# The retention stage of a two-block transformer kernel, rebuilt

## The chip, the cores and the metric

One NeuronCore of a Trainium2 chip runs the whole kernel in one launch. The metric is device time in microseconds; the median of three runs of the kernel before is 1687.16 us (1682.4 to 1688.15).

## What is computed

The reference applies two blocks to 256 tokens of width 1024, batch 1, in float32. The first has two layers (grouped plus dilated attention, then latent attention, each with an MLP); the second has two layers with SwiGLU feeds around a mixer: differential attention, then retention. The change is in the retention:

```
def _retention(xn, w_in, subln, w_out):        # 4 heads, Dk 256, Dv 512
    q, k, v, g = split(xn @ w_in)
    ...                                        # chunks of 128; over all 256 tokens the same as:
    # o[q] = sum over keys <= q of (q.k / 16) * gamma**(q - key) * v[key]
    o = _rms(o, subln)                         # over the 512 of a head
    return (silu(g) * o) @ w_out
x1 = h + 0.5 * _swiglu(_rms(h, ...), ...)      # feed "swi2" ends here
m  = _retention(_rms(x1, mix_norm), ...)       # norm 8 of the kernel, then "rt_in", "rt_out"
x2 = x1 + m                                    # norm 9, feed "swi3"
```

## The kernel before

All weights are packed on the host into 267 slabs of 128 x 2048 float32 (1 MB each). SyncE brings them in order into a ring of six (`raw`), as subtractions free its places. Each slab is split into a high part `whi` (ScalarE cast to fp32r, L236) and a low part `wlo` (VectorE subtraction, L240), rings of three. `split_high(m)` waits until slab m - 3 is used up. Activations are split the same way (`xh`, `xl`), and every product is taken as three fp32r matmuls (`three`, L246 to L248). An input slab holds 256 output columns, 48 matmuls of 256 columns; an output slab holds 256 rows of the second matrix, 24 matmuls of 512 columns into the four `accs` banks. The engines run their lists in the order in which the code is written, coupled by semaphores; there is no scheduler.

Between two stages stands a norm, numbered q. In a "raw" norm (q in `RAW_Q`) the residual times the gain is transposed and split at once, the root of the mean square is worked out beside it, and the scale is applied later (`scale_out`, `rstd`). Norm 8 is not one of them: `scale_block` (L579) waits for the root, multiplies, and only then PE transposes (`turn_part`, L481); `first_slabs` starts the retention's first slab by features. `last_slabs` is the end of a stage's output slabs; in raw norms it takes six more matmuls of the older slab before it waits for the newest operand. Norm 5, ahead of the attention stage `da_in`, is raw and starts with `first_tokens` (tokens as rows).

`rt_in` has 24 slabs, six per head: q, k, two of v, two of g. `rt_tensor` projects each into one of six PSUM banks, q, k and g with features as rows, v with tokens as rows; VectorE copies q, k, v out (L2339, L2342), ScalarE takes Silu of g (L2325). The first head's rest is written out, the other three are a loop. When all 24 are done, `ret_tensor` starts. For each head u: `scores` (fp32, L2355), VectorE multiplies by the decay table (`decayed`, L2443), 12 products of 128 columns with v (L2402) that give o with features as rows, ScalarE squares (L2421), PE sums over features with a column of ones (L727), ScalarE takes the root (L2424), PE spreads it along the rows (L734), VectorE scales, applies the gate and splits (L2454, L2457, L2465, L2472), PE runs two output slabs (`out_`). Head u + 1's products and scores stand ahead of head u's output slabs in PE's list. The last two output slabs go through `last_slabs`.

## Time and profile before

| | |
|---|---|
| runs | 1687.16, 1688.15, 1682.4 us |
| the profiled execution | 1686.48 us, its span 1684.7 us |
| granted TensorE clock, mean | 0.992 |
| busy share of PE, DVE, ACT | 98%, 63%, 50% |
| chain of waits that ended last | PE 86%, DVE 7%, ACT 4% |

PE is TensorE's matmuls, DVE VectorE, ACT ScalarE, POOL GpSimd. A busy share is a mean over all stages; what one stage is limited by is seen only in windows and timelines of that stage. One fp32 matmul shows as two records on PE, an fp32r matmul or a transpose as one. Records overlap their neighbours, so the pace of a row of matmuls is read from their starts.

### The profile page before, as it was taken

The numbers are of one execution on the slowest core, as the hardware profiler recorded it, in microseconds if no ns is written. First come the engines' busy times: TensorE is split into PE (matmuls) and PEld (weight loads), VectorE is DVE, ScalarE is ACT, GpSimd is POOL, SyncE is SP. The second block draws the span as 40 slices with busy tenths as digits, with TensorE's granted clock in tenths as the row PEclk, the third lists the DMA queues.
The fourth block names the chain that finished last, engine by engine and source line by source line (L and its number), as shares of the span: only waits on it lengthen the run. The fifth ranks groups of instructions, "written<-read, shape, count | busy, mean of one in ns | idle before, by whom it ended". The sixth has DMA issues, their size and how long they took to land.

```text
span 1684.7 us, 24578 instructions
## 1 busy us (share of the span) xinstructions
PE 1648.3 (98%) x9684; PEld 1418.1 (84%) x9686; DVE 1061.4 (63%) x1214; ACT 846.4 (50%) x1046; POOL 32.1 (2%) x44
## 2 busy tenths in 40 slices
PE   8999999999999999999999999999999998999999
PEld 7878888758888788889888888888888998878887
DVE  6766655766665666666777666666666454566665
ACT  5654444665444454446775544544444443345443
POOL 2000000000000000000100000000000000000000
PEclk9999999999999999999999999999999999999999
DMA  9525545323554454544344545454544443335540
GB/s 368 193 116 214 179 192 200 120 92 123 203 191 182 175 191 184 200 186 176 126 163 172 212 178 200 165 210 187 195 179 169 178 189 126 125 114 212 191 183 25
DMA packets 42714, 294.19 MB, mean 175 GB/s; under 512 B 4736, under 2 KB 5040, under 8 KB 8592
## 3 DMA queue, kind: packets, MB, share of 16 engines
q1 hardware_dynamic: 39168, 281.04, 44.2%
q0 software_dynamic: 2752, 10.58, 1.8%
q10 hardware_dynamic: 720, 1.51, 0.2%
q8 instruction: 56, 0.92, 0.2%
q14 instruction: 18, 0.15, 0.0%
HBM read 289.96 MB, written 3.15 MB: 174 GB/s over the span
## 4 chain that ended last, share of the span: by engine, by line
PE 86%; DVE 7%; ACT 4%; issue 2%; DMA 1%; SPq 0%; DVEq 0%; ACTq 0%
PE ups L267 25%; PE accs L246 11%; PE accs L248 11%; PE accs L247 11%; PE ups L265 11%; DVE wlo L240 2%; PE ups L248 2%; PE ups L247 2%; PE ups L246 2%; PE ups L270 2%; ACT whi L236 1%; DVE h L719 1%; DMA raw<-weights 1%; PE ups L2402 1%; PE ups L432 1%
## 5 line engine op out<-in xcount | busy, mean ns | idle before, releaser
L240 DVE TENSOR_TENSOR wlo<-raw,whi 128x2048 fp32r<-128x2048 f32 x265 | 609.1, 2300 | 206.8 <-ACT whi L236 206.8
L267 PE MATMUL ups<-xhl,whi 128*128 128x512 f32 x1824 | 634.1, 396 | 0.0
L236 ACT CAST whi<-raw 128x2048 fp32r<-128x2048 f32 x265 | 505.3, 1909 | 113.1 <-PE accs L248 60.6
L265 PE MATMUL ups<-xhl,wlo 128*128 128x256 f32 x1596 | 445.0, 279 | 0.0
L267 PEld LDWEIGHTS ups<-xhl,whi 128*128 128x128 f32 x1824 | 331.0, 188 | 64.1
L265 PEld LDWEIGHTS ups<-xhl,wlo 128*128 128x128 f32 x1596 | 300.9, 189 | 10.1
L246 PE MATMUL accs<-whi,hidh 128*128 128x512 f32 x660 | 259.3, 393 | 1.7 <-DVE hidl L895 1.7
L248 PE MATMUL accs<-whi,hidl 128*128 128x512 f32 x660 | 257.2, 390 | 0.0
L247 PE MATMUL accs<-wlo,hidh 128*128 128x512 f32 x660 | 257.1, 390 | 0.0
L246 PEld LDWEIGHTS accs<-whi,hidh 128*128 128x128 f32 x660 | 124.0, 188 | 26.8 <-issue 4.5
L248 PEld LDWEIGHTS accs<-whi,hidl 128*128 128x128 f32 x660 | 124.0, 188 | 26.4
L247 PEld LDWEIGHTS accs<-wlo,hidh 128*128 128x128 f32 x660 | 124.1, 188 | 25.5
L246 PE MATMUL accs<-whi,xhl 128*128 128x256 f32 (+1 forms) x368 | 120.9, 329 | 4.2 <-DVE xhl L2472 2.6
L869 DVE TENSOR_TENSOR hid<-ups,hid 128x512 f32<-128x512 f32 x70 | 48.4, 691 | 121.5 <-ACT hid L842 68.2
L248 PE MATMUL accs<-whi,xhl 128*128 128x256 f32 (+1 forms) x368 | 116.9, 318 | 0.0
L247 PE MATMUL accs<-wlo,xhl 128*128 128x256 f32 (+1 forms) x368 | 116.7, 317 | 0.0
L850 ACT CAST hidh<-hid 128x512 fp32r<-128x512 f32 x76 | 47.2, 621 | 128.0 <-DVE hid L893 75.8
L842 ACT COPY hid<-ups 128x512 f32<-128x512 f32 x44 | 25.7, 585 | 131.1 <-PE ups L267 131.1
L895 DVE TENSOR_TENSOR hidl<-hid,hidh 128x512 fp32r<-128x512 f32 x76 | 52.6, 693 | 52.2 <-ACT hidh L850 52.2
L246 PEld LDWEIGHTS accs<-whi,xhl 128*128 128x128 f32 x368 | 70.4, 191 | 12.7 <-issue 3.9
L248 PEld LDWEIGHTS accs<-whi,xhl 128*128 128x128 f32 x368 | 70.3, 191 | 4.8
L847 ACT COPY sub_rstd<-ups 128x512 f32<-128x512 f32 x44 | 25.7, 584 | 96.2 <-PE ups L267 96.2
(282 smaller groups left out, 2022.1 us busy)
## 6 DMA issues: line engine op xcount, KB each, us to landing
raw<-weights SPq DMA_DIRECT2D x265, 1024.0 KB, 4.8
gain<-gains POOLq DMA_DIRECT2D x9, 512.0 KB, 4.0
rel_scratch<-sub_rstd POOLq DMA_DIRECT2D x1, 2048.0 KB, 17.6
big<-rel_scratch POOLq DMA_DIRECT2D x1, 1536.0 KB, 9.4
h<-x_in SPq DMA_DIRECT2D x2, 512.0 KB, 6.8
raw<-weights SPq DMA_DIRECT2D x2, 512.0 KB, 10.3
tabs<-consts POOLq DMA_DIRECT2D x1, 1024.0 KB, 7.7
gain<-gains ACTq DMA_DIRECT2D x1, 512.0 KB, 5.1
```

The costliest lines, as they stand in the source:

```text
L236: nc.scalar.copy(whi[:, m % SPLIT, :], raw[:, m % RAW, :]).then_inc(hi_ready, 1)
L240: nc.vector.tensor_tensor(wlo[:, m % SPLIT, :], raw[:, m % RAW, :], whi[:, m % SPLIT, :].bitcast(F32), ALU.subtract).then_inc(lo_ready, 1)
L246: nc.tensor.matmul(out_ap, sh, mh, start=first, stop=False)
L247: nc.tensor.matmul(out_ap, sh, ml, start=False, stop=False)
L248: return nc.tensor.matmul(out_ap, sl, mh, start=False, stop=last)
L265: nc.tensor.matmul(bank[:, 0:T], W(wlo, n, k, j * P, (j + 1) * P), xh[:, k, :], start=False, stop=False)
L267: mm = nc.tensor.matmul(bank, W(whi, n, k, j * P, (j + 1) * P), xhl[:, :, k, :], start=k == 0, stop=k == KC - 1)
L270: nc.tensor.matmul(bank[:, 0:T], W(wlo, n, k, j * P, (j + 1) * P), xh[:, k, :], start=False, stop=False)
L842: nc.scalar.copy(flat2(slot), sum_parts(0)[0 if begin else 1]).then_inc(S("feed_side"), 1)
L850: nc.scalar.copy(hidh[:, g % per, :, :].rearrange("p a n -> p (a n)"), slot).then_inc(S("feed_hidden_high"), 1)
L869: nc.vector.tensor_tensor(flat2(part), sum_parts(second)[0], flat2(part), ALU.add).then_inc(S("feed_sum"), 1)
L895: nc.vector.tensor_tensor(hidl[:, g % per, :, :].rearrange("p a n -> p (a n)"), slot, hidh[:, g % per, :, :].rearrange("p a n -> p (a n)") ...
```

## The change

- Norm 8 is raw and of the token kind (`RAW_Q`, `TOKEN_Q`), so `first_slabs` goes and `first_tokens` starts the stage. Since k and v then lack the norm's scale, v is multiplied by the reciprocal of the mean square (`rt_square`); q's scale falls out of the head's own norm, whose epsilon is scaled instead (`eps_raw`); the gate's Silu takes `rstd` as its scale.
- A head's slabs now come as v, v, q, k, g, g. v and g are projected with tokens as rows, q and k with features as rows, into the four `accs` banks in turn.
- Scores stand between the halves of the head's fifth slab and the value products between the halves of the sixth. The products are three of 512 columns, with o's tokens as rows, into `up[2]` and `up[3]`.
- ScalarE's Square accumulates the sum over the row (no matmuls for sum and spread). `gated` multiplies o by root and gate in one instruction per token block.
- Eight pairs of 128-feature blocks are transposed (`turn_pair`), three between halves of slabs 8, 9 and 14, five between halves of output slabs 0 to 4; ScalarE takes the high part with the gain as scale, DVE the low part.
- The loops over heads are written out on all three engines.

In the diff new functions are whole; of removed ones only the first lines stand.

```diff
@@ -72,8 +72,8 @@
-PLAIN_NORMS = (4, 9)
-ROOT_NORMS = (0, 2, 5, 6, 7, 8, 10)
+PLAIN_NORMS = (4,)
+ROOT_NORMS = (0, 2, 5, 6, 7, 8, 9, 10)
...
@@ -329,25 +329,6 @@
-        def first_slabs(pe, n, q):
...
@@ -458,10 +439,10 @@
-        TOKEN_Q = (2, 5)
-        RAW_Q = (0, 1, 2, 3, 4, 5, 6, 7, 9)
+        TOKEN_Q = (2, 5, 8)
+        RAW_Q = (0, 1, 2, 3, 4, 5, 6, 7, 8, 9)
...
-        SCALES = [0, "ab_eps", 1, 2, "c_eps", 3, 5, 6, "eps", 7, 8, 10]
+        SCALES = [0, "ab_eps", 1, 2, "c_eps", 3, 5, 6, "eps", 7, 8, 9, "r_eps", 10]
...
@@ -722,10 +703,6 @@
-        def sum_tokens(dst, squares, heads, first=True, last=True):
...
@@ -743,7 +720,7 @@
-        ROWS = {"swi0": 1, "swi1": 2, "swi2": 3, "swi3": 4 + RT_HEADS}
+        ROWS = {"swi0": 1, "swi1": 2, "swi2": 3, "swi3": 4}
...
@@ -2295,186 +2263,233 @@
+        n_ro = FIRST["rt_out"]
+        RT_SLABS = 6
+        q_rt, k_rt = big[:, 0:2 * T], big[:, 2 * T:4 * T]
+        att_rt = hid
+        v_rt, gate_rt = (big[:, at * T:(at + 8) * T].rearrange("p (s t n) -> p s t n", s=2, t=TB) for at in (4, 12))
+        on_rt = big[:, 20 * T:36 * T].rearrange("p (u t n) -> p u t n", u=RT_HEADS, t=TB)
+        rt_junk = xn[:, 0:4 * T].rearrange("p (t n) -> p t n", t=TB)
+        rt_square = sb("rt_square", [P, TB])
+        rt_sums = sb("rt_sums", [P, TB])
+        RT_PAIRS = 2 * RT_HEADS
+        def rt_bank(m):
+            return accs[:, m % 4, :]
+        def rt_high(c):
+            return hidh[:, (c % 14) // 2, c % 2, :] if c % 14 < 6 else xh[:, c - 6, :]
+        def rt_low(c):
+            return hidl[:, (c % 14) // 2, c % 2, :] if c % 14 < 6 else xl[:, c - 6, :]
+        def rt_features(s):
+            return (lambda k: rt_high(2 * s + k)), (lambda k: rt_low(2 * s + k))
+        def pair_bank(p):
+            return up[1] if p < 3 or p % 2 else up[0]
...
         def rt_tensor(pe):
...
+            def bank_free(m):
+                if m >= 4:
+                    u, j = (m - 4) // RT_SLABS, (m - 4) % RT_SLABS
+                    if j < 2:
+                        pe.wait_ge(S("rt_v"), 2 * u + j + 1)
+                    else:
+                        pe.wait_ge(S("rt_taken"), 4 * u + j - 1)
+            def half_slab(m, half_):
+                n, j = n_r + m, m % RT_SLABS
+                if half_ == 0:
+                    pe.wait_ge(lo_ready, n + 1)
+                    bank_free(m)
+                if j in (2, 3):
+                    mm = project_features(n, rt_bank(m), (half_,))
+                else:
+                    mm = project_tokens(n, rt_bank(m), blocks=(half_,))
+                if half_ == 1:
...
-        def ret_tensor(pe):
             def scores(u):
+                pe.wait_ge(S("rt_taken"), 4 * u + 2)
+                if u >= 1:
+                    pe.wait_ge(S("r_decayed"), u)
...
+                        mm = nc.tensor.matmul(up[0][:, kb * T + kb * P:(kb + 1) * T],
+                                              k_rt[:, c * T + kb * P:c * T + (kb + 1) * P],
+                                              q_rt[:, c * T + kb * P:(c + 1) * T], start=c == 0, stop=c == 1)
...
-            def sum_squares(u):
...
+            def values(u):
+                pe.wait_ge(S("r_decayed"), u + 1)
+                pe.wait_ge(S("rt_v"), 2 * u + 2)
+                if u >= 1:
+                    pe.wait_ge(S("r_gated"), u)
...
-            def spread_root(u):
...
+                    for kb in range(t + 1):
+                        at = kb * T + t * P
+                        mm = nc.tensor.matmul(up[2 + t], att_rt[:, u % 2, at:at + P], v_rt[:, u % 2, kb, :],
+                                              start=kb == 0, stop=kb == t)
+                mm.then_inc(S("r_values"), 1)
+            def turn_pair(p):
+                u = p // 2
+                pe.wait_ge(S("r_gated"), u + 1)
+                if p >= 1:
+                    pe.wait_ge(S("r_low"), p if p < 4 else p - 1)
+                for c in range(2):
+                    at = (2 * (p % 2) + c) * P
+                    for t in range(TB):
+                        mm = nc.tensor.transpose(pair_bank(p)[:, c * T + t * P:c * T + (t + 1) * P],
+                                                 on_rt[:, u, t, at:at + P], ident)
+                mm.then_inc(S("r_turned"), 1)
+            for m in range(RT_HEADS * RT_SLABS):
+                u, j = m // RT_SLABS, m % RT_SLABS
+                if m == 0:
+                    first_tokens(pe, n_r, 8, rt_bank(0)).then_inc(slab_used, 1)
+                else:
+                    half_slab(m, 0)
+                    if j == 4:
+                        scores(u)
+                    if j == 5:
+                        values(u)
+                    if m in (8, 9, 14):
+                        turn_pair((8, 9, 14).index(m))
+                    half_slab(m, 1)
+            for s in range(6):
+                n = n_ro + s
+                pe.wait_ge(lo_ready, n + 1)
+                pe.wait_ge(S("r_low"), s + 1)
+                if s == 0:
+                    pe.wait_ge(S("rt_taken"), 4 * RT_HEADS - 2)
+                project_out(n, *rt_features(s), first=s == 0, blocks=(0,))
+                if s == 0:
+                    pe.wait_ge(S("rt_taken"), 4 * RT_HEADS)
+                if s < 5:
+                    turn_pair(s + 3)
+                project_out(n, *rt_features(s), first=s == 0, blocks=(1,)).then_inc(slab_used, 1)
+            pe.wait_ge(S("r_low"), 7)
+            last_slabs(pe, n_ro + 6, rt_features(6), rt_features(7), 9,
+                       ready=lambda: pe.wait_ge(S("r_low"), RT_PAIRS))
+        def rt_scalar(act):
+            def stats(u):
+                act.wait_ge(S("r_values"), u + 1)
...
-            def out_(u):
...
+                    ins = nc.scalar.activation(rt_junk[:, t, :], up[2 + t], ACT.Square, accum_out=rt_sums[:, t:t + 1])
+                ins.then_inc(S("r_sq"), 1)
+                if u == 0:
+                    act.wait_ge(S("scale_ready"), SCALES.index("r_eps") + 1)
+                act.wait_ge(S("r_sq"), u + 1)
...
+                    act.wait_ge(S("r_rstd"), u)
+                for t in range(TB):
+                    ins = nc.scalar.activation(std8[:, 0, t:t + 1], rt_sums[:, t:t + 1], ACT.Sqrt,
+                                               bias=eps_raw[:, t:t + 1], scale=1.0 / RT_DV)
+                ins.then_inc(S("r_std"), 1)
+            def high_pair(p):
+                act.wait_ge(S("r_turned"), p + 1)
+                if p == RT_PAIRS - 1:
+                    act.wait_ge(slab_used, n_ro + 1)
+                for c in range(2):
+                    ins = nc.scalar.activation(rt_high(2 * p + c), pair_bank(p)[:, c * T:(c + 1) * T], ACT.Copy,
+                                               scale=cols[:, G_RT + 2 * p + c:G_RT + 2 * p + c + 1])
+                ins.then_inc(S("r_high"), 1)
+            raw_root_scalar(act, 9)
+            for m in range(RT_HEADS * RT_SLABS):
+                u, j = m // RT_SLABS, m % RT_SLABS
+                split_high(act, n_r + m + 2)
+                if j == 1 and u >= 1:
+                    stats(u - 1)
+                if j in (2, 3):
+                    act.wait_ge(slab_used, n_r + m + 1)
+                    if u >= 1:
+                        act.wait_ge(S("r_scores"), u)
+                    nc.scalar.copy((q_rt, k_rt)[j - 2], rt_bank(m)).then_inc(S("rt_taken"), 1)
+                if j in (4, 5):
+                    act.wait_ge(slab_used, n_r + m + 1)
+                    if m == 4:
+                        act.wait_ge(rstd_ready, ROOTS[9] + 1)
+                    if u >= 2:
+                        act.wait_ge(S("r_gated"), u - 1)
...
-        def ret_scalar(act):
...
-        def ret_vector(dve):
+                        ins = nc.scalar.activation(gate_rt[:, u % 2, t, (j - 4) * T:(j - 3) * T],
+                                                   rt_bank(m)[:, t * T:(t + 1) * T], ACT.Silu,
+                                                   scale=rstd[:, t:t + 1])
+                    ins.then_inc(S("rt_taken"), 1)
+                if m in (8, 9, 14):
+                    high_pair((8, 9, 14).index(m))
+            stats(RT_HEADS - 1)
+            for s in range(5):
+                split_high(act, n_ro + s + 2)
+                high_pair(s + 3)
+            split_high(act, n_ro + 7)
+            split_high(act, n_ro + 8)
+        def rt_vector(dve):
...
+                    ins = nc.vector.tensor_tensor(att_rt[:, u % 2, sl], up[0][:, sl], decay[:, u, sl], ALU.mult)
...
+            def gated(u):
+                dve.wait_ge(S("r_std"), u + 1)
+                nc.vector.reciprocal(rstd8[:, 0, 0:TB], std8[:, 0, 0:TB]).then_inc(S("r_rstd"), 1)
+                dve.wait_ge(S("r_rstd"), u + 1)
+                dve.wait_ge(S("rt_taken"), 4 * u + 4)
+                for t in range(TB):
+                    ins = nc.vector.scalar_tensor_tensor(on_rt[:, u, t, :], up[2 + t], rstd8[:, 0, t:t + 1],
+                                                         gate_rt[:, u % 2, t, :], ALU.mult, ALU.mult)
+                ins.then_inc(S("r_gated"), 1)
+            def low_pair(p):
+                dve.wait_ge(S("r_high"), p + 1)
+                for c in range(2):
+                    ins = nc.vector.scalar_tensor_tensor(rt_low(2 * p + c), pair_bank(p)[:, c * T:(c + 1) * T],
+                                                         cols[:, G_RT + 2 * p + c:G_RT + 2 * p + c + 1],
+                                                         rt_high(2 * p + c).bitcast(F32), ALU.mult, ALU.subtract)
+                ins.then_inc(S("r_low"), 1)
+            raw_root(dve, 9)
+            dve.wait_ge(half_ready, STATS[9] + 3)
+            nc.vector.tensor_scalar(eps_raw[:, :], mean_eps[:, 1, :], EPS, None, ALU.mult
+                                    ).then_inc(S("scale_ready"), 1)
+            nc.vector.reciprocal(rt_square[:, :], mean_eps[:, 1, :]).then_inc(S("r_square"), 1)
+            dve.wait_ge(S("r_square"), 1)
...
+            for m in range(RT_HEADS * RT_SLABS):
+                u, j = m // RT_SLABS, m % RT_SLABS
+                split_low(dve, n_r + m + 2)
+                if j < 2:
+                    dve.wait_ge(slab_used, n_r + m + 1)
+                    if u >= 2:
+                        dve.wait_ge(S("r_values"), u - 1)
+                    for t in range(TB):
+                        ins = nc.vector.tensor_scalar(v_rt[:, u % 2, t, j * T:(j + 1) * T],
+                                                      rt_bank(m)[:, t * T:(t + 1) * T], rt_square[:, t:t + 1], None,
+                                                      ALU.mult)
+                    ins.then_inc(S("rt_v"), 1)
+                if j == 1 and u >= 1:
+                    gated(u - 1)
+                if j == 4:
+                    decayed(u)
+                if m in (8, 9, 14):
+                    low_pair((8, 9, 14).index(m))
+            gated(RT_HEADS - 1)
+            for s in range(5):
+                split_low(dve, n_ro + s + 2)
+                low_pair(s + 3)
+            split_low(dve, n_ro + 7)
...
@@ -2596,8 +2611,6 @@
-            bring_table(ACT.Sqrt)
-            ret_scalar(act)
...
@@ -2623,7 +2636,6 @@
-            ret_vector(dve)
...
@@ -2644,7 +2656,6 @@
-            ret_tensor(pe)
...
@@ -2776,7 +2787,7 @@
-        slabs += [w[hd], w[4 + hd], w[8 + 2 * hd], w[9 + 2 * hd], w[16 + 2 * hd], w[17 + 2 * hd]]
+        slabs += [w[8 + 2 * hd], w[9 + 2 * hd], w[hd], w[4 + hd], w[16 + 2 * hd], w[17 + 2 * hd]]
...
```

Where it moves instructions, PE first, at head 0's value products, in the order of its list (`hid` holds the decayed scores, `big` q and v, `xn` k). Before, all of a head stands behind the last projected slab:

```order
L2355 MATMUL ups<-big,xn 128x256 [waits rt_gated,rt_free]
L2355 MATMUL ups<-big,xn 128x256
L2355 MATMUL ups<-big,xn 128x128 x2
L2402 MATMUL ups<-hid,big 128x128 [waits r_decayed]
L2402 MATMUL ups<-hid,big 128x128 x11
L2355 MATMUL ups<-big,xn 128x256 x2
L2355 MATMUL ups<-big,xn 128x128 x2
L727 MATMUL ups<-mats,sub_rstd 128x1 [waits r_sq]
L727 MATMUL ups<-mats,sub_rstd 128x1
L727 MATMUL ups<-mats,sub_o 128x1 x2
L727 MATMUL ups<-mats,sub_rstd 128x1 x2
L727 MATMUL ups<-mats,sub_o 128x1 x2
```

After, the products stand between the two halves of the sixth slab (L246 to L248 are its projection):

```order
L247 MATMUL accs<-wlo,xhl 128x256
L248 MATMUL accs<-whi,xhl 128x256
L2334 MATMUL ups<-big,hid 128x512 [waits rt_v,r_decayed]
L2334 MATMUL ups<-big,hid 128x512 x2
L246 MATMUL accs<-whi,xhl 128x256
L247 MATMUL accs<-wlo,xhl 128x256
```

The scores have moved ahead by one slab, the sums (L727) and the spread root (L734) are gone, and the 12 products are 3. The first transposes stand likewise, in the middle of slab 8:

```order
L247 MATMUL accs<-xhl,whi 128x256
L248 MATMUL accs<-xhl,wlo 128x256
L2346 MATMUL ups<-mats,big 128x128 [waits r_gated]
L2346 MATMUL ups<-mats,big 128x128 x3
L246 MATMUL accs<-xhl,whi 128x256
```

ScalarE, at head 0's statistics. Before:

```order
L2421 ACTIVATE sub_rstd<-ups 128x512 [waits r_values]
L2421 ACTIVATE sub_o<-ups 128x512
L2424 ACTIVATE std<-ups,eps 128x2 [waits r_sum]
L2432 CAST xhl<-sub_rstd 128x512 [waits r_gate]
L2432 CAST xhl<-sub_o 128x512
L236 CAST whi<-raw 128x2048 [waits slab_used,raw_loaded5]
```

After, with slab conversions (L236) on both sides, the table load for Sqrt, and behind it the copy of q (L2415) and the high part of pair 0 (L2401):

```order
L236 CAST whi<-raw 128x2048 [waits slab_used,raw_loaded0]
L2384 ACTIVATE xn,rt_sums<-ups 128x512 [waits r_values]
L2384 ACTIVATE xn,rt_sums<-ups 128x512
L2392 ACT_TABLE_LOAD [waits r_sq]
L2392 ACTIVATE std<-rt_sums,eps_raw 128x1 [waits scale_ready]
L2392 ACTIVATE std<-rt_sums,eps_raw 128x1
L236 CAST whi<-raw 128x2048 [waits slab_used,raw_loaded1]
L2415 COPY big<-accs 128x512 [waits r_scores,slab_used]
L2401 ACTIVATE hidh<-ups,cols 128x256 [waits r_turned]
L2401 ACTIVATE hidh<-ups,cols 128x256
```

The Squares now give the sums themselves, nothing waits for PE between them and the root, and the casts of later slabs stand behind them in ScalarE's list.

## Rows read from the trace of the kernel before

**Rows 1.** The page, busy time by engine.
```profile
PE 1648.3 (98%) x9684; PEld 1418.1 (84%) x9686; DVE 1061.4 (63%) x1214; ACT 846.4 (50%) x1046; POOL 32.1 (2%) x44
```

**Rows 2.** Windows: stretch, length, busy of PE, PEld, DVE, ACT, POOL; clock, DMA, GB/s.
```profile
763.62:773.28 9.66, 9.66 (x43) 7.70 (x42) 6.94 (x7) 5.66 (x7) 0.00 (x0) 1.00 0.39 149
763.62:782.73 19.11, 18.81 (x113) 16.35 (x112) 14.65 (x18) 12.32 (x17) 0.00 (x0) 1.00 0.30 118
782.73:794.25 11.52, 11.52 (x98) 11.52 (x97) 7.53 (x14) 5.94 (x9) 0.00 (x0) 1.00 0.68 242
1257.46:1281.54 24.08, 22.11 (x124) 17.28 (x124) 15.18 (x19) 14.81 (x20) 0.53 (x1) 1.00 0.31 112
1281.54:1414.02 132.48, 132.48 (x1106) 132.44 (x1104) 65.36 (x48) 56.51 (x37) 0.00 (x0) 1.00 0.50 190
1414.02:1482.70 68.68, 61.53 (x355) 54.12 (x353) 35.48 (x55) 24.33 (x30) 0.00 (x0) 0.95 0.30 104
1427.00:1432.00 5.00, 4.98 (x24) 5.00 (x25) 3.29 (x5) 2.94 (x3) 0.00 (x0) 0.51 0.00 0
1482.70:1494.07 11.37, 11.37 (x43) 8.94 (x43) 4.80 (x4) 1.67 (x4) 0.00 (x0) 0.85 0.28 111
```

**Rows 3.** Timeline of PE at norm 8: start, length, instruction, idle before it.
```profile
1261.22 0.47 PE L246 MATMUL accs<-whi,hidh 128*128 128x512 f32 x1 [0.88 <-DVE hidl L895]
...
1268.83 0.33 PE L481 MATMUL ups<-mats,xn 128*128 128x128 f32 x1 [0.54 <-DVE xn L579]
```

**Rows 4.** Timeline of PE in the retention.
```profile
1417.39 2.94 PE L2402 MATMUL ups<-hid,big 128*128 128x128 f32 x24 [0.79 <-DVE hid L2443]
1420.17 1.47 PE L2355 MATMUL ups<-big,xn 128*128 128x256 f32 x8
...
1427.02 5.23 PE L2402 MATMUL ups<-hid,big 128*128 128x128 f32 x24 [2.30 <-DVE sub_o L2457]
1432.09 1.47 PE L2355 MATMUL ups<-big,xn 128*128 128x256 f32 x8
1433.32 0.47 PE L246 MATMUL accs<-whi,xhl 128*128 128x512 f32 x1
...
1482.70 0.50 PE L246 MATMUL accs<-whi,xhl 128*128 128x512 f32 x1 [2.64 <-DVE xhl L2472]
```

**Rows 5.** Groups of PE by line and shape: count, busy us, mean ns; then line 1327.
```profile
L2355 PE MATMUL ups<-big,xn 128*128 128x256 f32 x16 | 4.2, 384 | 0.9 <-ACT big L2325 0.9
L2355 PE MATMUL ups<-big,xn 128*128 128x128 f32 x16 | 2.4, 274 | 0.0
...
L1327 PE MATMUL ups<-sub_rstd,rel_sb x2: 587/640/692, 26.2 to 26.7; 32*128 32x512 f32 x2
```

**Rows 6.** Timeline of PE at norm 5's last transposes.
```profile
779.42 0.60 PE L481 MATMUL ups<-mats,xn 128*128 128x128 f32 x4
779.77 0.36 PE L361 MATMUL accs<-whi,xhl 128*128 128x256 f32 x1
```

**Rows 7.** Groups of ACT, then DVE, 1281.54 to 1494: count, busy us, mean ns, idle.
```profile
L236 ACT CAST whi<-raw 128x2048 fp32r<-128x2048 f32 x30 | 57.1, 1902 | 60.2 <-PE ups L248 52.3 <-PE accs L248 7.9
...
L2421 ACT ACTIVATE sub_rstd<-ups 128x512 f32<-128x512 f32 x4 | 2.4, 592 | 5.1 <-PE ups L2402 5.1
...
L240 DVE TENSOR_TENSOR wlo<-raw,whi 128x2048 fp32r<-128x2048 f32 x31 | 71.0, 2291 | 50.9 <-ACT whi L236 50.9
L2342 DVE COPY big<-ups 128x256 f32 x16 | 6.1, 420 | 13.1 <-PE ups L248 13.1
L2457 DVE SCALAR_TENSOR_TENSOR sub_rstd<-ups,cols,hid 128x256 f32<-128x256 f32 x8 | 3.5, 480 | 0.1
...
L719 DVE SCALAR_TENSOR_TENSOR h<-accs,h 128x512 f32<-128x512 f32 x1 | 0.7, 685 | 0.0
```

**Rows 8.** Timeline of ACT at the first gate.
```profile
1304.87 1.28 ACT L2325 ACT_TABLE_LOAD   x1 [3.95 <-PE accs L248]
1306.17 0.60 ACT L2325 ACTIVATE big<-accs 128x512 f32 x1
```

More of the change, by code:

```diff
@@ L721, in add_piece @@
                 factor, h[:, t, lo:hi], ALU.mult, ALU.add).then_inc(h_ready, 1)
-        def sum_tokens(dst, squares, heads, first=True, last=True):
-            return nc.tensor.matmul(dst, squares, heads, start=first, stop=last)
         def spread(dst, column):
@@ L2317, in rt_scalar @@
-        def rt_scalar(act):
-            act.sem_inc(S("rt_gated"), 2)
-            with act.Fori(0, RT_HEADS) as i:
-                for j in range(6):
-                    n = n_r + j
-                    split_high(act, n + 2, i)
-                    if j >= 4:
-                        act.wait_ge(slab_used, after(n + 1, i, RAW))
-                        nc.scalar.activation(big[:, bass.ds(i * (4 * T) + (24 + 2 * (j - 4)) * T, 2 * T)],
-                                             BANKS6[j], ACT.Silu).then_inc(S("rt_gated"), 1)
```

150 lines of the change are left out of this document (removed).

## The prediction

> **What bounds the kernel now.** I read the page first: TensorE (PE) holds 98% of the span, so anything that changes the time has to shorten PE's own queue, either its work or its stalls [rows 1]. A busy share does not say which, so the second view is the table of windows, cut where PE passes from one stage to the next [rows 2]. Its first three rows are the attention stage's norm (for comparison), the others the stretch that the change rebuilds: norm 8 with the first slab of the projections (24.08 us), the other 23 slabs (132.48 us), retention and the first six output slabs (68.68 us), and the last two output slabs up to the next norm's first transpose (11.37 us). Together they are 1257.46 to 1494.07, 236.61 us. The third view is PE's timeline at the seams and inside the retention [rows 3, 4]. The reader is to see three things there.
>
> The 23 slabs are dense: 132.48 us are 23 times 5.76, and 5.76 is 48 matmuls of 256 columns at 0.120 each. Nothing can be won in them, but much can be put beside them: over those 132.48 us DVE is busy 65.36 and ScalarE 56.51 [rows 2].
>
> The retention is not dense. PE waits 0.79 us for `hid` before head 0's products and 2.30 us for the normed values before head 1's; head 3's output starts after 2.64 us of waiting for `xhl` [rows 4]. After both of the long waits the granted clock is at 1.2 instead of 2.4 GHz: 0.51 of full in 1427 to 1432, and 0.85 on average over 1482.70 to 1494.07 [rows 2]. The 24 records of head 1's products take from 1427.02 to 1432.09, 5.07 us, those of head 0 from 1417.39 to 1420.17, 2.78 us [rows 4].
>
> Norm 8 is the one norm of the feeds that multiplies by the root before it transposes, and its `last_slabs` has the short form of the order: PE stands 0.88 us for the last hidden part there, and 0.54 for the scaled `xn` ahead of its first transposes [rows 3].
>
> **The norm.** With 8 in RAW_Q and TOKEN_Q, norm 8 runs the code of norm 5, which has the same kind of feed ahead, the same `scale_out` in its add and `first_tokens` behind. Norm 5 takes 19.11 us from the start of `last_slabs` to the start of the second projected slab; norm 8 now takes 24.08 for the same way [rows 2]. Gain 4.97. The root and the two reciprocals then stand on ScalarE and DVE ahead of slab 2's conversion. That cast (1.90) and subtraction (2.29) start at the latest when slab 0 is done and need 4.2 us; slab 2 starts 5.76 us later, so they are covered.
>
> **The 24 slabs.** Same 48 matmuls each. Before, the six slabs of a head are a loop on PE; now they are written out. The attention stage's slabs are written out too and run 96 matmuls in 11.52 us, 0.120 each [rows 2], so I keep 132.48.
>
> **What goes between the halves of slabs.** All of it adds to PE's queue.
> - Scores: 4 per head as before. 1432.09 to 1433.32 is 1.23 us; for the first matmul after each inserted piece I allow 0.1. 4 x 1.33 = 5.3 us.
> - Value products: 3 of 512 columns instead of 12 of 128 per head, two records each. The trace has no such matmul at 128 rows, so its cost is bounded. Records of 128 and 256 columns last 0.274 and 0.384 [rows 5], 0.110 more for 128 more columns; those of 128 are issued 0.116 apart (24 in 2.78), so 512 columns give 0.116 + 3 x 0.110 = 0.446, and 6 of them 2.7 us with nothing more: an estimate from those rows. From below: 512 columns at the fp32r pace, 9.66 us for 42 of them, 0.23 each [rows 2], 1.4 us a head. From above: the only 512-column fp32 record, 0.640 mean at 32 rows [rows 5], not overlapped at all, 3.8 us. I take 2.7 since the two shapes beside it are on one line, plus 0.1 for the restart: 4 x 2.8 = 11.2 us (ends 6.0 and 15.6). Before they were 2.7 to 2.8 at full clock, so the wider product by itself wins next to nothing.
> - Transposes: 32 in 8 groups of four, new. A group in norm 5 takes 779.42 to 779.77, 0.35, and 0.09 allowed for the restart [rows 6]: 8 x 0.44 = 3.5 us.
>
> The Trainium skill has a rule that bears on the wide product. "TensorE: Matmul & The Clock Gate", Back-to-back issue gap, gives N/2.4 + 2.5 ns a pass for a warm stream, and "FP8 and Floating Point Precision", TensorE Precision Notes, four passes for true FP32. By it a head's products are 12 x 0.216 = 2.59 us in the new form and 48 x 0.056 = 2.68 in the old, an estimate. The trace's old form, 2.78, agrees with it within 4%; by these pages of the Trainium skill the sum would be some 0.4 us lower.
>
> **The output.** Six whole output slabs of 24 matmuls of 512 columns, at 9.66/42 = 0.230: 6 x 5.52 = 33.1 us; then `last_slabs` as in norm 5, 9.66 us [rows 2].
>
> **What goes.** The waits and the two stretches at half clock, and on PE the sums of squares and the spreading of the root, which for head 0 lie between its products at 1417.39 and head 1's at 1427.02 [rows 4]. ScalarE's Square accumulates that sum instead.
>
> **Sum.** 19.11 + 132.48 + 5.3 + 11.2 + 3.5 + 33.1 + 9.66 = 214.3 us against 236.61: 22.3 us less. The profiled execution took 1686.48 us (span 1684.7), so 1664.2; the median of the three runs, 1687.16, is 0.68 above it. Forecast 1665 us.
>
> **What hides the rest, and what is late next.** Per head ScalarE has 6 casts (11.4), two copies out of PSUM and two Squares at 0.59 (2.4, with 0.4 for the accumulator reads, my allowance), 4 Silu and 4 high parts of 256 columns (0.42 each, between half of 0.59 and all of it: 3.4), two table loads (2.6) and two roots (0.5): 20.7 us. DVE has 6 subtractions (13.7), 4 value scalings at 0.42 (1.7), decay (0.7), two gatings at 0.69 (1.4), 4 low parts at 0.48 (1.9): 19.4 [rows 7]. A head lasts 34.56 + 1.33 + 2.8 + 0.9 = 39.6 on PE. What is late next is order, not load, at three places.
> 1. PE's transposes in slab 8 and 14 wait for `r_gated` of the head before. The gating stands behind the value scaling of slab 7, which needs slab 7 finished: 0.2 + 0.84 + 0.2 (reciprocal) + 1.4 = 2.6 us into slab 8. PE arrives at 2.88. Margin 0.2; the two latencies of 0.2 are allowances of mine. If it is missed, some tenths twice.
> 2. Pair 1 is transposed in the middle of slab 9 and waits for pair 0's low part: ScalarE copies q (0.2 to 0.8), takes the high part (to 1.6), DVE the low part (to 2.6). Again 2.88 for PE.
> 3. After slab 23, ScalarE has the gate (to 1.0), Squares (2.6), table load and root (4.4), then the cast of output slab 2 (6.3); DVE is done with it at 8.6. PE needs that slab two output slabs and one group later, at 11.3. Queued behind that cast are pair 3 and the other casts; pair 3 is wanted at output slab 3, at 17. Cover 2.7 us.
>
> Row and rule differ on the table load. In the rows a load takes 1.28 us, and the activation behind it starts 0.02 us after its end [rows 8]. The Trainium skill, "ScalarE: Activation LUTs", What ACT_TABLE_LOAD costs, adds a drain of 1.38 for about 2.66 us a switch, and its rules for authors say to group by table set, while this change alternates Sqrt and Silu for every head. By the Trainium skill's figure the cast in place 3 is 1.4 us later, inside its cover.
>
> **Rivals.**
> A (forecast, 87%): PE runs through. 1665; for this case alone 1659 to 1670: the value products' ends (-5, +4) and the runs' spread.
> B (8%): the in-order queues miss places 1 to 3, and a wait of the size of those seen drops the clock again. For: margins of 0.2 us, and ScalarE casts stand behind waits for PE. Against: one miss delays only tenths. Price: two waits of 2.5 us and 2.3 us at half clock behind each (5.07 less 2.78): 9.6, so 1675.
> C (2%): table switches are on the path after all, each delaying a cast that PE waits for: 8 x 1.28 = 10.2 gives 1675. By the figure of the Trainium skill's page on ScalarE it would be 8 x 2.66 = 21, 1686.
> D (3%, slower): the granted clock falls at the seams between projection and small fp32 work. Place: the 4 scores, 4 products and 8 groups of transposes, 16 seams. Price: 2.3 us for each, what head 1's products lost (5.07 less 2.78), 37 us if all do: 1702. It decides from 10 of the 16. For: both falls of the trace are in this stage. Against: both stand behind waits of over 2 us [rows 2, 4], and norm 5's window with 12 and 4 transposes in it has a clock of 1.00 [rows 2].
> The change might also not do what it says: the wide products do not win anything, by the working above, and the gain is that of the waits and the norm. That is in A.
>
> A measurement here tells about 0.3%, 5 us, from no change. Faster: A, B and C, with D's small end, 95%; within 0.3%: C or D at a good half of its full size, 2%; slower: D, 3%. The range 1656 to 1675 takes A with its bounds and most of B.
>
> **What would show it.** The stretch from the start of the feed's `last_slabs` to norm 9's first transpose is 214 us long instead of 236.6, no row of PE idle over 0.5 us inside it, granted clock 1.00 throughout. Right for the norm: 19.1 us to the second slab. Right for the products: six records 0.43 to 0.45 apart per head. Wrong: gaps ahead of `turn_pair` or of an output slab put down to ScalarE or DVE (B, C), a granted clock under 1.00 at the seams (D), or a saving elsewhere than in this stretch.

## The result

The changed kernel takes 1663.87 us (median of 4 runs, 1662.95 to 1666.92), the kernel before 1686.7 (4 runs, 1682.4 to 1688.15). The ratio is 0.9871, 95% interval 0.9855 to 0.9888: 1.3% faster. Forecast was 1665, range 1656 to 1675. The profiled execution has a span of 1661.5 us, before 1684.7: 23.2 less.

### The profile after

The page, busy time by engine and the chain of work that ended last:

```profile
PE 1634.5 (98%) x9553; PEld 1402.1 (84%) x9554; DVE 1050.1 (63%) x1198; ACT 852.5 (51%) x1079; POOL 32.0 (2%) x44
...
PE 89%; DVE 6%; ACT 3%; issue 2%; DMA 1%; ACTq 0%; DVEq 0%
```

Against [rows 1] the shares are the same to a per cent, and the kernel is 23 us shorter. PE's busy time fell by only 13.8 us, with 131 records fewer; the rest was idle time. (Busy time is not work: it holds matmuls on zeros and matmuls at half clock, as shown below.) The page cannot tell more, so the windows come next: last output slabs of the feed, norm 8 and the first projected slab; the other 23 slabs with all that now stands between their halves; six output slabs with five groups of transposes; the last two output slabs.

```profile
1257.75:1276.86 19.11, 18.82 (x113) 16.35 (x112) 15.11 (x22) 11.58 (x18) 0.53 (x1) 1.00 0.44 143
1276.86:1426.14 149.28, 149.28 (x1175) 143.09 (x1173) 70.66 (x63) 69.94 (x77) 0.00 (x0) 1.00 0.48 173
1426.14:1461.20 35.06, 35.06 (x166) 28.99 (x165) 19.17 (x19) 19.09 (x25) 0.00 (x0) 1.00 0.46 164
1461.20:1470.85 9.65, 9.65 (x44) 7.70 (x42) 4.80 (x4) 3.16 (x4) 0.00 (x0) 1.00 0.64 217
```

Together 213.10 us where [rows 2] has 236.61: 23.5 less, so the whole gain lies in the stretch that the change rebuilds (it starts 0.29 us later than before, which is the rest). The clock is 1.00 in all four. In the three last ones PE's busy time is the window itself. The list of PE's waits over the whole stretch has one line (total us, times, longest), where before has eight waits, 8.96 us:

```profile
PE ups L462 <- DVE xn L577: 0.3, 1, 0.3
```

The value products of head 0 in PE's timeline:

```profile
1304.09 2.74 PE L2334 MATMUL ups<-big,hid 128*128 128x512 f32 x6
1306.27 0.68 PE L246 MATMUL accs<-whi,xhl 128*128 128x256 f32 x1
1306.79 0.28 PE L247 MATMUL accs<-wlo,xhl 128*128 128x256 f32 x1
```

The six records start 0.43 apart. The slab's next matmul is stretched to 0.68 and the one behind it starts 0.52 later instead of 0.12, so the piece costs 1306.79 - 1304.09 - 0.12 = 2.58 us a head.

The three places where the forecast saw thin margins. Place 1 and 2 first, on DVE (value scaling of slab 7, reciprocal, gating; low part of pair 0):

```profile
1321.26 0.88 DVE L2478 TENSOR_SCALAR big<-accs,rt_square 128x256 f32<-128x256 f32 x2 [1.48 <-PE accs L248]
1322.05 0.15 DVE L2447 RECIPROCAL rstd<-std 128x2 f32<-128x2 f32 x1
1322.24 1.41 DVE L2451 SCALAR_TENSOR_TENSOR big<-ups,rstd,big 128x512 f32<-128x512 f32 x2
...
1328.81 0.88 DVE L2458 SCALAR_TENSOR_TENSOR hidl<-ups,cols,hidh 128x256 fp32r<-128x256 f32 x2 [2.96 <-ACT hidh L2401]
```

and the transposes on PE that wait for them, with no idle time in front:

```profile
1323.94 0.60 PE L2346 MATMUL ups<-mats,big 128*128 128x128 f32 x4
...
1330.13 0.60 PE L2346 MATMUL ups<-mats,big 128*128 128x128 f32 x4
1330.49 0.36 PE L246 MATMUL accs<-xhl,whi 128*128 128x256 f32 x1
```

The gating ends at 1323.65, 0.29 ahead of PE; the low part at 1329.69, 0.44 ahead. At place 3 DVE splits output slab 2 at 1431.96 to 1434.25, and PE starts it at 1438.01: 3.8 us of cover.

```profile
1431.96 2.29 DVE L240 TENSOR_TENSOR wlo<-raw,whi 128x2048 fp32r<-128x2048 f32 x1 [0.19 <-ACT whi L236]
```

ScalarE's table loads, the first for the gate, the second for the root (Sqrt):

```profile
1296.75 1.28 ACT L2423 ACT_TABLE_LOAD   x1
1301.41 0.84 ACT L2423 ACTIVATE big<-accs,rstd 128x256 f32<-128x256 f32 x2 [3.38 <-PE accs L248]
...
1318.69 1.28 ACT L2392 ACT_TABLE_LOAD   x1
1319.99 0.48 ACT L2392 ACTIVATE std<-rt_sums,eps_raw 128x1 f32<-128x1 f32 x2
1321.31 1.90 ACT L236 CAST whi<-raw 128x2048 fp32r<-128x2048 f32 x1 [0.85 <-PE accs L248]
```

The gate's load is done while the activation still waits for PE; only the root's stands between two pieces of work, and the cast behind it still waits 0.85 for PE.

### The profile page after: what moved, and what is told of

Same layout as the page of the kernel before. It is cut to its first block, busy times and chain, and to the rows that moved or that the text cites. A ratio compares the mean times of both kernels' runs of the same rounds, so it can differ in the third digit from the quotient of the medians.

```text
span 1661.5 us, 24238 instructions
## 1 busy us (share of the span) xinstructions
PE 1634.5 (98%) x9553; PEld 1402.1 (84%) x9554; DVE 1050.1 (63%) x1198; ACT 852.5 (51%) x1079; POOL 32.0 (2%) x44
## 4 chain that ended last, share of the span: by engine, by line
PE 89%; DVE 6%; ACT 3%; issue 2%; DMA 1%; ACTq 0%; DVEq 0%
PE ups L267 26%; PE accs L246 14%; PE accs L248 13%; PE accs L247 13%; PE ups L265 11%; DVE wlo L240 2%; PE ups L270 2%; ACT whi L236 1%; DVE h L700 1%; PE ups L462 1%; PE ups L413 1%; PE ups L415 1%; PE ups L410 1%; PE ups L2334 1%; DMA mats<-consts 1%
## 5 line engine op out<-in xcount | busy, mean ns | idle before, releaser
L236 ACT CAST whi<-raw 128x2048 fp32r<-128x2048 f32 x265 | 505.1, 1909 | 79.7 <-PE accs L248 79.4
L246 PE MATMUL accs<-whi,hidh 128*128 128x512 f32 x692 | 272.1, 393 | 0.9 <-DVE hidl L872 0.9
L248 PE MATMUL accs<-whi,hidl 128*128 128x512 f32 x692 | 269.7, 390 | 0.0
L247 PE MATMUL accs<-wlo,hidh 128*128 128x512 f32 x692 | 269.6, 390 | 0.0
L246 PE MATMUL accs<-whi,xhl 128*128 128x256 f32 (+1 forms) x576 | 176.8, 307 | 1.6 <-DVE xhl L2184 1.6
L248 PE MATMUL accs<-whi,xhl 128*128 128x256 f32 (+1 forms) x576 | 171.6, 298 | 0.0
L247 PE MATMUL accs<-wlo,xhl 128*128 128x256 f32 (+1 forms) x576 | 171.4, 298 | 0.0
L248 PEld LDWEIGHTS accs<-whi,hidl 128*128 128x128 f32 x692 | 130.0, 188 | 27.7
L247 PEld LDWEIGHTS accs<-wlo,hidh 128*128 128x128 f32 x692 | 130.2, 188 | 26.6
L246 PEld LDWEIGHTS accs<-whi,hidh 128*128 128x128 f32 x692 | 130.1, 188 | 26.6 <-issue 3.3
L246 PEld LDWEIGHTS accs<-whi,xhl 128*128 128x128 f32 x576 | 110.0, 191 | 9.3 <-issue 4.9
L247 PEld LDWEIGHTS accs<-wlo,xhl 128*128 128x128 f32 x576 | 110.1, 191 | 3.7 <-issue 1.0
L248 PEld LDWEIGHTS accs<-whi,xhl 128*128 128x128 f32 x576 | 109.9, 191 | 3.3
```

The lines of the kernel that those rows point to most:

```text
L236: nc.scalar.copy(whi[:, m % SPLIT, :], raw[:, m % RAW, :]).then_inc(hi_ready, 1)
L246: nc.tensor.matmul(out_ap, sh, mh, start=first, stop=False)
L247: nc.tensor.matmul(out_ap, sh, ml, start=False, stop=False)
L248: return nc.tensor.matmul(out_ap, sl, mh, start=False, stop=last)
```

## The experiments

The theory: PE's queue sets the time. The gain is the sum of what left that queue (sums and spreads), of waits, of two stretches at half clock and of a shorter norm, and nothing else. (A spread is the matmul that puts a head's root into every row.) Rivals: the wide product is what pays; the table loads are on the path; the clock falls wherever small work meets slabs. Eight kernels, each with one change. The first starts from the kernel before, the others from the changed one. "Stretch" is always from the start of the feed's last output slabs to norm 9's first transpose, read from one profiled execution of each kernel: 236.61 us before, 213.10 after. In these comparisons the kernel before had medians of 1687.09 (experiments 1 to 4) and 1687.15 (5 to 8).

### 1. The kernel before, its two long waits filled with matmuls on zeros

```diff
+        def fill_wait(bank, count):
+            for _ in range(count):
+                nc.tensor.matmul(bank, zero[:, 0:P], zero[:, :], start=True, stop=True)
 ...                                  # ahead of the last two output slabs
+                if u == RT_HEADS - 1:
+                    fill_wait(up[0][:, :], 12)
 ...                                  # ahead of head 1's products
+                if u == 1:
+                    fill_wait(accs[:, 0, :], 10)
```

> The kernel before with two fillers: 10 bf16 matmuls of 512 columns ahead of head 1's products, 12 ahead of the last two output slabs, both inside waits that stay. Theory (the half clock follows PE's wait of over 2 us): head 1's products take 2.8 us instead of 5.07, the last output slabs lose no 1.85 us, together 4.1 us less than before (1682.5), granted clock 1.00 in both places, waits for the operands unchanged. Rival (the clock falls because of the small fp32 work itself, wait or not): products stay at 5 us and the time at 1686.

Measured: 1684.18 (10 runs), ratio to before 0.9979 (0.9965 to 0.9994). The stretch is 232.63, 3.98 less. In PE's timeline head 1's products come right behind the filling, and the windows over both places show full clock:

```profile
1425.54 2.11 PE L334 MATMUL accs<-zero 128*128 128x512 bf16 x9
1427.70 2.94 PE L2410 MATMUL ups<-hid,big 128*128 128x128 f32 x24
1430.49 1.47 PE L2359 MATMUL ups<-big,xn 128*128 128x256 f32 x8
```

```profile
1425.54:1432.00 6.46, 6.40 (x42) 4.97 (x42) 4.68 (x10) 2.99 (x4) 0.00 (x0) 1.00 0.00 0
1478.00:1483.00 5.00, 4.90 (x21) 2.73 (x22) 3.29 (x4) 3.04 (x4) 0.00 (x0) 1.00 0.60 210
```

1427.70 to 1430.49 is 2.79 us where [rows 4] has 5.07. The waits themselves are still there, filled. So the half clock behind the two waits was worth 4.0 us of the 23.5. The medians differ by 2.9 us; like all medians here they also hold what the clock does far ahead of the stretch (last section).

### 2. Norm 8 as before: the root multiplies first, both blocks are transposed before the first slab (which stays by tokens)

```diff
-PLAIN_NORMS = (4,)
+PLAIN_NORMS = (4, 9)
...
+            if q == 8:
+                turn_block(pe, q, 1)
...
-        RAW_Q = (0, 1, 2, 3, 4, 5, 6, 7, 8, 9)
+        RAW_Q = (0, 1, 2, 3, 4, 5, 6, 7, 9)
...
-                                                   scale=rstd[:, t:t + 1])
+                                                   scale=rt_square[:, t:t + 1])
...                                   # and both set to constants:
+            nc.vector.memset(rt_square[:, :], 1.0).then_inc(S("scale_ready"), 1)
+            nc.vector.memset(eps_raw[:, :], EPS).then_inc(S("scale_ready"), 1)
```

> The changed kernel with norm 8 as before: root first, scaled, both token blocks transposed before the first projection, short form of the last two output slabs. The rest of the stage as changed. Theory (norm 8 gave 4.97 us, apart from all else): 24.1 us from the start of the feed's last two slabs to the second projected slab instead of 19.1, the rest of the stretch as changed, 1668.9 us. Rival (the raw norm only moved the wait, or gave more by the order of the stage behind it): a stretch behind it that differs by over 0.5 us, or a time under 1667 or over 1671.

Measured: 1668.55 (6 runs), ratio 0.9902 (0.9876 to 0.9929). From the start of `last_slabs` to the second projected slab 23.75 us, the stretch 217.72: 4.62 more than the changed kernel. The medians say 4.7, which is partly chance: the six runs lie between 1663.17 and 1671.99, most likely for the reason told in the last section, and the profiled one is the shortest. The rest of the stretch is unchanged (149.26 and 44.71). The norm's share of the gain is 4.6 and adds to the others; the feature form of the first slab, which this edit does not bring back, is in the 24.08 us of before and not in these 23.75.

### 3. The same, with the second block transposed in the middle of the first slab

```diff
...                                   # in place of turn_block ahead of the slab
+            if q == 8:
+                turn_part(pe, q, 2)
```

> As the one before, but with the first slab by tokens: the first token block is projected while the root of the second is worked out. It tells what of the 5 us is the raw form and what the token form. Theory: 21.9 us to the second slab (2.8 more than the raw form, 2.2 less than the old), 1666.7 us. Rival (the raw form is all of it): 24 us and 1669. Other rival (the tokens are all of it): 19 us and 1664.

Measured: 1665.06 (4 runs), ratio 0.9875 (0.9846 to 0.9903); but in the trace the way to the second slab is 25.04 us, the stretch 219.10. Both the 21.9 us that was expected and the order between 2 and 3 failed. PE, and DVE before it:

```profile
1278.38 0.39 PE L246 MATMUL accs<-whi,xhl 128*128 128x256 f32 x1 [1.49 <-DVE wlo L240]
```

```profile
1269.35 1.42 DVE L562 SCALAR_TENSOR_TENSOR xn<-h,rstd,gain 128x512 f32<-128x512 f32 x2
1273.74 1.29 DVE L616 TENSOR_TENSOR xhl<-ups,xhl 128x512 fp32r<-128x512 f32 x2 [2.98 <-ACT xhl L493]
1276.03 2.29 DVE L240 TENSOR_TENSOR wlo<-raw,whi 128x2048 fp32r<-128x2048 f32 x1 [1.00 <-ACT whi L236]
```

The conversion of slab 1 stands behind the whole norm in both lists, and with the second block turned late it comes late: a wait of 1.49 us. Of the earlier waits only the one of 0.38 is gone; 0.88 and 0.52 are still there. In the changed kernel ScalarE casts slab 1 at 1270.10 and DVE subtracts at 1272.88, between the two halves of the norm. That this order is part of what the raw norm brings is read from these rows; no run moves the conversion alone. Why the median was low all the same is told in the last section: the stretch says 6.0 us, the medians 1.2, and the stretch is the better witness for one edit.

### 4. The value products as twelve of 128 columns

```diff
-                    for kb in range(t + 1):
-                        at = kb * T + t * P
-                        mm = nc.tensor.matmul(up[2 + t], att_rt[:, u % 2, at:at + P], v_rt[:, u % 2, kb, :],
+                    for c in range(4):
+                        for kb in range(t + 1):
+                            at = kb * T + t * P
+                            mm = nc.tensor.matmul(up[2 + t][:, c * P:(c + 1) * P], att_rt[:, u % 2, at:at + P],
+                                                  v_rt[:, u % 2, kb, c * P:(c + 1) * P],
```

> The changed kernel with 12 value products of 128 columns in place of 3 of 512, same place, same banks. Theory (cost goes by columns): 24 records at 0.107 to 0.116 with the restart, 2.7 to 2.8 us a head instead of 2.58, 0.8 us more in all, 1664.7. Rival (the width is what pays, since 4 times as many weight loads of 0.19 us come to light): 4.6 us a head, 8 us more, 1672.

Measured: 1663.66 (4 runs), ratio 0.985 (0.9821 to 0.9878); the changed kernel in its own comparison had 1663.87. The stretch is 213.52, 0.42 more, which is 0.10 a head:

```profile
1304.44 2.84 PE L2335 MATMUL ups<-big,hid 128*128 128x128 f32 x24
1307.04 0.36 PE L246 MATMUL accs<-whi,xhl 128*128 128x256 f32 x1
1307.24 0.28 PE L247 MATMUL accs<-wlo,xhl 128*128 128x256 f32 x1
```

24 records of 128 columns in 2.60, the next start 0.08 late: 2.68 against 2.58. The rival that the wide product pays is out: it gives 0.4 us in all. What it brings is its layout, with o's tokens as rows, in which the sum of squares runs along a row.

### 5. Scores directly ahead of the products

```diff
-                    if j == 4:
-                        scores(u)
                     if j == 5:
+                        scores(u)
                         values(u)
```

> The changed kernel with the scores moved one slab back, directly ahead of the value products. Theory (placing them between halves of slabs hides the decay's latency, and a wait under 2 us leaves the clock alone): PE waits 0.8 to 1.0 us for VectorE's decayed scores in each head, one restart of 0.1 less, 3.5 us more in all, 1667.4, clock 1.00. Rival (each such wait also costs clock): 2.3 us more each, 1677. Other rival (nothing was hidden by the place): 1664.

Measured: 1668.23 (4 runs), ratio 0.9884 (0.9854 to 0.9915). The stretch is 217.02, 3.92 more. PE waits for DVE's decay product once per head, four times 0.71:

```profile
1304.29 1.47 PE L2321 MATMUL ups<-big 128*128 128x256 f32 x8
1306.47 2.84 PE L2334 MATMUL ups<-big,hid 128*128 128x512 f32 x6 [0.71 <-DVE hid L2441]
```

```profile
1303.00:1311.00 8.00, 7.29 (x43) 5.55 (x42) 2.82 (x3) 1.25 (x1) 0.00 (x0) 1.00 0.33 119
```

2.84 us of waits, and 0.27 a head for stopping and starting again. The clock stays at 1.00 through these four waits.

### 6 and 7. More table loads for each head, two and four

```diff
+                for r in range(1):        # 7: range(2)
+                    for c, function in enumerate((ACT.Sqrt, ACT.Silu)):
+                        at = 4 * u + 2 * r + c
+                        nc.scalar.activation(table_more[:, at:at + 1], eps[:, :], function)
```

They stand between the Squares and the root.

> The changed kernel with two more table loads (Sqrt, Silu, each with an activation of one column) in each head's statistics, 3.0 us later root. Theory (ScalarE's load is covered except at two tight places): the gating before the transposes of slabs 8 and 14 ends 1.35 us later, of which 0.29 are covered, 1.1 us of wait twice; output slab 2's conversion is 3 us later inside its cover of 3.7; 2.1 us more, 1666.0. Rival C (each load is on the path): 8 more loads x 1.28 = 10.3 us, 1674; with a drain of 1.38 behind each load 21 us.

> The same with four more loads, the root 5.9 us later. Theory: the transposes of slabs 8 and 14 wait 4.0 us each, output slab 2 waits 2.3 us for its conversion, and behind each of the three waits a stretch at half clock costs up to 2.3 us: 10 to 17 us more, 1674 to 1681. Rival (ScalarE's load is covered by the slabs in any place): 1664 to 1666. Rival C: 16 loads x 1.28 = 20.5, 1684.

Measured: two more, 1666.22 (4 runs), ratio 0.9873 (0.985 to 0.9897), stretch 215.60; four more, 1680.04 (10 runs), ratio 0.996 (0.9946 to 0.9974), stretch 229.33. ScalarE in the second one:

```profile
1318.32 1.28 ACT L2393 ACT_TABLE_LOAD   x1
1319.62 0.20 ACT L2393 ACTIVATE table_more<-eps 128x1 f32<-128x1 f32 x1
1319.82 1.28 ACT L2393 ACT_TABLE_LOAD   x1
1321.12 0.20 ACT L2393 ACTIVATE table_more<-eps 128x1 f32<-128x1 f32 x1
```

A load and its small activation take 1.50 us together, so two more are 3.0 and four are 6.0 us later. PE ahead of the transposes of slab 8, with two and with four, and PE's windows behind its three waits in the latter:

```profile
1328.90 0.66 PE L2347 MATMUL ups<-mats,big 128*128 128x128 f32 x4 [1.07 <-DVE big L2456]
```

```profile
1327.80 1.12 PE L2347 MATMUL ups<-mats,big 128*128 128x128 f32 x4 [4.08 <-DVE big L2456]
```

```profile
1327.80:1332.00 4.20, 4.20 (x20) 4.20 (x21) 2.29 (x1) 0.09 (x1) 0.00 (x0) 0.50 0.13 31
1373.50:1376.50 3.00, 2.99 (x15) 2.99 (x16) 2.29 (x1) 0.10 (x1) 0.00 (x0) 0.53 0.00 0
1452.16:1455.00 2.84, 2.84 (x7) 2.26 (x8) 2.84 (x3) 2.67 (x4) 0.00 (x0) 0.51 0.53 159
```

3.0 - 1.07 and 6.0 - 4.08 are both 1.9: that is the slack of the changed kernel on ScalarE's side, of which 0.29 is the visible margin and the rest the time for which the finished root lies there while DVE scales v. With two more, PE waits 1.07 and 1.02 us, the clock stays at 1.00, and the stretch grows by 2.5. With four more, PE waits 4.08, 4.03 and 2.16 (for output slab 2, whose cover was 3.8: 6.0 - 3.8 = 2.2), 10.3 us; behind each of the three the clock is at 1.2 GHz, and the stretch grows by 16.2, so the half clock, with the restarts, adds 5.9, some 2.0 for each. The medians say 2.35 and 16.2. Twice as many loads cost over six times as much.

### 8. The old sums and the spread root, put back on PE as work that nobody reads

```diff
+            def old_sums(u):
...
+                for t in range(TB):
+                    for c in range(4):
+                        nc.tensor.matmul(up[1][:, t:t + 1], v_rt[:, u % 2, t, c * P:(c + 1) * P], ones[:, 0:1],
+                                         start=c == 0, stop=c == 3)
+                for t in range(TB):
+                    spread(up[1][:, T + t * P:T + (t + 1) * P], ones[:, t:t + 1])
...
+                        old_sums(u)       # behind values(u)
```

> The changed kernel with the old form's sum of squares and spread put back on PE as work without use: per head 8 fp32 products of one column and 2 of 128, behind the value products; nothing waits for them. Theory (on a dense PE every matmul counts in full): 1.70 + 0.36 + 0.1 us a head, 8.6 us more, 1672.5. Rival (these one-column products hide beside their neighbours): under 3 us more, 1666.

Measured: 1672.26 (4 runs), ratio 0.9913 (0.9888 to 0.9937). The stretch is 221.99, 8.89 more, with not one wait more:

```profile
1306.81 1.84 PE L2343 MATMUL ups<-mats,big 128*128 128x1 f32 x16
1308.52 0.69 PE L711 MATMUL ups<-mats 128*128 128x128 f32 x4
1308.96 0.36 PE L246 MATMUL accs<-whi,xhl 128*128 128x256 f32 x1
```

16 records of one column take 1.71 us from start to start, four of 128 columns 0.44. One column costs 0.107 a record, hardly less than the 0.108 of 128 columns in experiment 4. This is the largest single line of the gain; the waits and the half clock behind two of them are more when taken together (11.2 us).

## Why the prediction was right

**The ledger.** Of the 23.5 us:

| part | us | from |
|---|---|---|
| norm 8 and first slab | 5.0 | 24.08 to 19.11; experiment 2: 4.6 |
| waits of PE in the retention | 7.2 | 8.96 less the 1.80 in norm 8, none left |
| half clock behind two of them | 4.0 | experiment 1 |
| sums and spread off PE | 8.9 | experiment 8, in the new place |
| products | 0.4 | experiment 4 |
| transposes, new | -3.5 | 8 x 0.44 |
| not separated | 1.5 | difference |

The last line is what the retention lost besides at its many stops; experiment 5 shows 0.27 for each wait, and five waits there are gone. That is an argument, not a measurement. The line of the waits is a reading of two traces: no run puts the products back behind the slabs, but experiments 5 and 7 show that a wait put back costs at least its own length. The loops that were written out show no gain in the 23 slabs, which were dense before; in the retention nothing separates them from the last line.

**The total.** The stretch carries it: forecast 214.3, measured 213.10. That the profiled executions before and after both had half clock near 352 and 590 us, far ahead of the stretch, is luck; experiment 2's had it at neither place and reached the stretch 4.7 us earlier.

**Norm.** Forecast 19.11, measured 19.11. The same code behind the same kind of feed gave the same time, with one wait of 0.3 us in both; the reasoning from the sister stage was the safest of the whole sum. What it gave as the reason (waits of 0.88 and 0.54) is the smaller part. It overlooked a row of the kernel before:

```profile
1271.38 2.54 PE L330 MATMUL ups<-zero 128*128 128x512 bf16 x11
1274.30 1.32 PE L481 MATMUL ups<-mats,xn 128*128 128x128 f32 x8 [0.38 <-DVE xn L579]
```

Ahead of a norm that is not raw, `last_slabs` ends with `stay_warm`: twelve matmuls on zeros (11 in the record) that fill PE's wait for the root and count as busy. The window of norm 8 has 124 records before and 113 after, 11 fewer. The filled wait with the 0.38 behind it is 2.92 us (1271.38 to 1274.30); with 0.88 and 0.54 it makes 4.34, less the 0.29 that is left: 4.05 of the 4.97 us. So this gain too is mostly a wait, one that the list of waits does not show. The other 0.9 us is not separated. Experiments 2 and 3 have the same row of zeros, so the 4.6 us of experiment 2 hold it.

**23 slabs, scores, transposes, output.** Window 2 is 149.28 = 132.48 + 5.3 + 10.3 + 3 x 0.44 within 0.1; scores are 1.22 and 0.09 a head (1.33 forecast), a group of transposes 0.36 and 0.08 (0.44). Window 3 is 35.06, forecast 33.1 + 2.2; window 4 is 9.65, forecast 9.66.

**Products.** The step that was off: forecast 4 x 2.8 = 11.2, measured 4 x 2.58 = 10.3. The pace is 0.43 a record, not 0.446, and six times 0.43 is the whole 2.58: the 0.1 for the restart does not show behind the wide products. The step makes up 0.9 of the 1.2 us by which 214.3 was too high. The Trainium skill ("TensorE: Matmul & The Clock Gate", Wait — 56ns, not 53.3ns?, with the four passes of "FP8 and Floating Point Precision", TensorE Precision Notes) gives 2.59 and 2.68 for the two forms, an estimate that holds no restart. Measured without the restart they are 2.58 and 2.60: the trace agrees within 3%, and these pages were nearer for the wide form than my estimate from two row lengths. The section that the prediction names for it, Back-to-back issue gap of the same page of the Trainium skill, calls it the gap of an isolated matmul.

**The three places.** Margins 0.29, 0.44 and 3.8 where 0.2, 0.3 and 2.7 were forecast, on the same waits. Nothing was missed, so rival B did not happen; experiments 6 and 7 show that its mechanism is real. 1.9 us more on ScalarE would have used up the margin of place 1, in slab 8 and in slab 14, and 6 us more brings the clock down too and misses place 3; place 2 was missed in neither. The price set for B, 2.3 us of half clock behind a long wait, is confirmed within 0.3 us (2.0).

**Rival C, tables on the path.** No: the gate's loads are done ahead of their wait, and behind the root's loads 1.9 us of slack are left. The root's activation starts 0.02 us after the end of its load, in the changed kernel and in experiment 7, where four loads in a row are 1.50 apart with an activation of 0.20 between them. The drain of 1.38 us that the Trainium skill adds ("ScalarE: Activation LUTs", What ACT_TABLE_LOAD costs) shows in no row here; by it the four loads would have put PE 5.5 us further back than they did, an estimate (4 x 1.38). The measurement decides: a switch costs 1.28.

**Rival D, clock at the seams.** Refuted: 16 seams, all at 1.00. In experiment 1 the half clock went when the two waits were filled, with the small work left as it was.

**The chances.** A, B and C are 97% as rivals, but 95% together with a part of D in the split by outcome; one of the two is mis-added. It changes nothing in the forecast time.

## What to carry to other kernels

When one engine is 98% busy, look first at what its busy rows are: here one of them was filler in a wait. Then write its queue out as a sum of pieces with start-to-start times from the nearest sister stage; such a sum came within 1.2 us in 214. An fp32 matmul of one column cost PE as much here as one of 128 (0.107 and 0.108 us a record), so sums over partitions and broadcasts are worth moving to an engine that accumulates along its rows, if the layout can be turned at low cost (here 3.5 us of transposes against 8.9 us of sums and spreads). Then look for slack behind each wait: in the rebuilt stage waits of 1.0 us cost some 1.25 us each, and those of 2.16 to 4.08 us some 2.0 us of clock on top of their own length.

## What the runs showed of the hardware that was not expected

**The clock falls behind the same wait in one execution and not in another.** Far ahead of the change, at 352 us, PE waits 1.93 us in the changed kernel and in experiment 2, in the same code. The rows are the wait and the window behind it, first in the changed kernel, then in experiment 2:

```profile
352.38 0.65 PE L1378 MATMUL ups<-mats,xn 128*128 128x128 f32 x4 [1.93 <-DVE xn L1674]
```

```profile
354.00:360.00 6.00, 6.00 (x23) 3.12 (x21) 2.94 (x9) 1.99 (x6) 0.00 (x0) 0.50 0.01 3
```

```profile
352.20 0.66 PE L1381 MATMUL ups<-mats,xn 128*128 128x128 f32 x4 [1.93 <-DVE xn L1677]
```

```profile
354.00:360.00 6.00, 6.00 (x43) 4.14 (x43) 4.19 (x14) 3.65 (x12) 0.00 (x0) 1.00 0.01 3
```

A second place, near 590 us, behind a wait of 2.04 us, behaves alike. From the row at 352 us to the start of the feed's last slabs it is 905.37 us with both at half clock and 900.83 with neither, so these two are worth 4.5 us. Experiment 6's execution has a third place: behind a wait of 1.49 us that ends at 328.88 its clock is 0.50 in 332 to 334 us, where the changed kernel, after the same wait, has 1.00. This fits the spread of the runs, of which only one of each kernel has a trace: experiment 4 took 1663.65 to 1664.07 at a mean clock of 0.995 and once 1658.88 at 0.999; experiment 2 took 1671.72 and 1671.99 at 0.993, 1663.17 and 1663.65 at 0.999 and 0.998. Three of the four runs of experiment 3 were at 0.998 or 0.999, the fourth at 0.995 and 4 us longer, which fits its low median. The Trainium skill ("TensorE: Matmul & The Clock Gate", Part 1: The HAM clock gate) says of cold starts that their count of slow matmuls varies from run to run; the traces show the same for falls in the middle of a kernel. For one small edit compare the stretch, not the totals. In this case's traces waits of 0.3 to 1.5 us in the rebuilt stage left the clock up; those of 1.49, 1.93 and 2.04 elsewhere did and did not, so a wait's length alone does not decide; and the five of 2.16 to 4.08 in the rebuilt stage (before, and experiment 7) were followed by half clock each time.

**A table load can run ahead of the wait.** The gate's load is done at 1298.03, while its activation starts 3.38 us later, when PE's matmuls are finished. All four gate loads do so, so half of this stage's eight loads take no time from the work behind them. Before, the first gate's load came only after the wait [rows 8]; what decides it was not tried.
